# Reading the residual times the norm weight in the first two chunks of four feed-forward stages, and applying the root behind the product

## What is computed

```
def rms_norm(x, g):
    y = x32 * lax.rsqrt(jnp.mean(x32 * x32, axis=-1, keepdims=True) + EPS)
    return (y * g.astype(jnp.float32)).astype(x.dtype)
def modulate(h, shift, scale):
    return h * (1.0 + scale[:, None, :]) + shift[:, None, :]
def swiglu(h, wg, wu, wd):
    return (jax.nn.silu(h @ wg) * (h @ wu)) @ wd

# second block, layer i (the first block has no modulate and no g)
h = modulate(rms_norm(x, ln_ffn1[i]), sh1, sc1)
x = x + 0.5 * g1[:, None, :] * swiglu(h, ffn1_wg[i], ffn1_wu[i], ffn1_wd[i])
...
h = modulate(rms_norm(x, ln_ffn2[i]), sh3, sc3)
x = x + 0.5 * g3[:, None, :] * swiglu(h, ffn2_wg[i], ffn2_wu[i], ffn2_wd[i])
x = rms_norm(x, ln_out[i])
```

## Time and profile before

| what | value |
|---|---|
| median of 3 runs | 1580.49 us (1580.12 to 1580.62) |
| the profiled execution | 1580.53 us, of which the span from the first to the last instruction is 1578.6 us |
| PE busy | 1536.8 us, 97% of the span |
| DVE busy | 1183.6 us, 75% |
| ACT busy | 795.3 us, 50% |
| mean granted clock of PE | 0.989 |

### The profile page before, as it was taken

How to read it: one execution, slowest core, us unless ns; L and a number is a source line. 1 busy time by engine, 2 the same in 40 slices (tenths; PEclk the granted TensorE clock), 3 DMA queues, 4 the chain that set the end, 5 groups by cost and what they waited for, 6 DMA issues and landing times.

```text
span 1578.6 us, 27180 instructions
## 1 busy us (share of the span) xinstructions
PE 1536.8 (97%) x10710; PEld 1417.8 (90%) x10710; DVE 1183.6 (75%) x1435; ACT 795.3 (50%) x931; POOL 13.0 (1%) x33
## 2 busy tenths in 40 slices
PE   6999999899999999999999899999999999999998
PEld 6999998699999999999888799998999989999997
DVE  4788889967888868888867678888655566765555
ACT  5444464464444574444566654445544456454443
POOL 1000000000000000000000000000000000000000
PEclk8999999799999999999999999999999999999999
DMA  6988854238888448888453488886555544545551
GB/s 215 350 310 303 291 159 149 93 127 293 293 303 305 164 156 302 313 303 301 137 165 107 130 278 305 299 286 206 182 182 185 179 164 146 187 160 186 186 186 53
DMA packets 244680, 341.05 MB, mean 216 GB/s; under 512 B 5891, under 2 KB 188315, under 8 KB 244624
## 3 DMA queue, kind: packets, MB, share of 16 engines
q1 hardware_dynamic: 242656, 334.72, 62.3%
q0 software_dynamic: 1968, 5.54, 1.0%
HBM read 339.17 MB, written 2.63 MB: 217 GB/s over the span
## 4 chain that ended last, share of the span: by engine, by line
PE 90%; DVE 5%; ACT 3%; issue 1%; DMA 1%; SPq 0%; DVEq 0%; ACTq 0%
PE banks L1400 26%; PE banks L1365 15%; PE banks L1367 14%; PE banks L1366 14%; PE banks L1401 13%; DVE arena L1081 2%; PE banks L1390 1%; PE banks L1386 1%; DVE w_lo L847 1%; PE banks L1511 1%; ACT w_hi L451 1%; PE banks L1387 1%; PE banks L1454 1%; DMA raw<-in_ffn_w_in 1%; DVE xn L1012 0%
## 5 line engine op out<-in xcount | busy, mean ns | idle before, releaser
L847 DVE TENSOR_TENSOR w_lo<-raw,w_hi 128x2048 fp32r<-128x2048 f32 x245 | 560.2, 2288 | 150.9 <-ACT w_hi L451 150.8
L1400 PE MATMUL banks<-xs,w_hi 128*128 128x512 f32 x1728 | 613.1, 399 | 0.0
L451 ACT ACTIVATE w_hi<-raw 128x2048 fp32r<-128x2048 f32 x245 | 466.7, 1907 | 65.1 <-PE banks L1367 48.0
L1401 PE MATMUL banks<-xs,w_lo 128*128 128x256 f32 x1728 | 485.5, 281 | 0.0
L1400 PEld LDWEIGHTS banks<-xs,w_hi 128*128 128x128 f32 x1728 | 324.9, 188 | 78.4
L1401 PEld LDWEIGHTS banks<-xs,w_lo 128*128 128x128 f32 x1728 | 326.6, 189 | 0.0
L1365 PE MATMUL banks<-gu_hi,w_hi 128*128 128x256 f32 x960 | 274.3, 286 | 0.0
L1367 PE MATMUL banks<-gu_hi,w_lo 128*128 128x256 f32 x960 | 271.7, 283 | 0.0
L1366 PE MATMUL banks<-gu_lo,w_hi 128*128 128x256 f32 x960 | 271.6, 283 | 0.0
L933 DVE SCALAR_TENSOR_TENSOR ada_acc<-ada,c_act,ada_acc 128x512 f32<-128x512 f32 x252 | 189.1, 750 | 7.7
L1365 PE MATMUL banks<-xs,w_hi 128*128 128x256 f32 x640 | 185.4, 290 | 1.0 <-DVE xs L854 1.0
(11 more groups left out here) (258 smaller groups left out, 1821.5 us busy)
## 6 DMA issues: line engine op xcount, KB each, us to landing
ada<-in_ada_w SPq DMA_DIRECT2D x72, 1024.0 KB, 5.0
raw<-in_ffn_w_in SPq DMA_DIRECT2D x44, 1024.0 KB, 6.5
raw<-in_ffn_wg SPq DMA_DIRECT2D x44, 1024.0 KB, 5.3
raw<-in_ffn_wu SPq DMA_DIRECT2D x44, 1024.0 KB, 5.2
raw<-in_ffn_wd SPq DMA_DIRECT2D x44, 1024.0 KB, 4.9
raw<-in_ffn_w_out SPq DMA_DIRECT2D x22, 1024.0 KB, 6.1
raw<-in_attn_w_qkv SPq DMA_DIRECT2D x12, 1024.0 KB, 5.1
raw<-in_w_in SPq DMA_DIRECT2D x10, 1024.0 KB, 5.2
```

The costliest lines, as they stand in the source:

```text
L451: act.activation(w_hi[:, s, :], raw[:, s, :], ACT.Copy).then_inc(hi_ready, 1)
L847: dve.tensor_tensor(w_lo[:, s, :], raw[:, s, :], w_hi[:, s, :].bitcast(F32), ALU.subtract)\
L1400: pe.matmul(o, wh[:, k, m], pair[:, :, k, :], start=(k == 0), stop=False, skip_group_check=True)
L1401: ins = pe.matmul(o[:, 0:T], wl[:, k, m], pair[:, 0, k, :], start=False, stop=(k == KT - 1), skip_group_check=True)
```

## The change

In stages 2, 7, 9 and 11 (`DEFER`) the chunks `c0` and `c0+1` no longer read the normed activation but `u`, which is the residual tile times its norm weight, split into high and low in `xs`. ACT makes `xs_hi` straight from `x` (Identity with the weight column as scale and a column of zeros as bias), tile by tile between its squares, and DVE makes `xs_lo` (`u_low`) in the stage before. PE takes `c0` first and the sums of squares after it, into banks 0 and 1; the filling products are gone in these stages. The root is applied at the banks: DVE multiplies the bank of `c0` into `silu_g` and that of `c0+1` into `gu` (`u_scale`). Where there is a shift (stages 7, 9, 11), the `xs` tiles carry two more columns with it, so that the matmuls of these two chunks have 258 columns and the product of shift and weight comes out in column 256 of each bank; DVE copies it to `u_bias`, and it is added inside Silu and inside the product of gate and up. Then the normed tiles are made as before, for the chunks from `c0+2` on, each `xs_hi` tile once PE has read the old one in `c0+1`. `split(c0+2)` moves ahead of the root on both engines, `split(c0+3)` too on ACT, while on DVE `split(c0+3)` stands behind the eight tiles and the second `u_scale`; `split(c0+1)` of DVE moves behind `u` and the sums of squares; the renormed residual of stage 9 moves behind the second gate times up. The rows of `xs` become 258 words for every stage.

```diff
+DEFER = (2, 7, 9, 11)
...
-        xs = sb("xs", [P, 2, KT, T], F32R)
-        xs_hi, xs_lo = xs[:, 0], xs[:, 1]
+        xs = sb("xs", [P, 2, KT, T + 2], F32R)
+        xs_hi, xs_lo = xs[:, 0, :, 0:T], xs[:, 1, :, 0:T]
+        u_bias = sb("u_bias", [P, 2, 2, 1])
...
+        U_TILES = [banks8[:, i:i + 2, 0:T] for i in (4, 6)]
+        U_SHIFTS = [banks8[:, i:i + 2, T:T + 1] for i in (4, 6)]
...
@@ ACT, norm(n)
+                    if d is not None:
+                        scale, shift = norm_cols(d)
+                        if shift is not None:
+                            act.wait_ge(x_ready, 8 * (n - 1) + 1)
+                            act.activation(xs[:, 0, :, T:T + 2], shifts(d), ACT.Copy)
+                        for k in range(KT):
+                            act.wait_ge(x_ready, 8 * (n - 1) + k + 1)
+                            act.activation(xs_hi[:, k, :], x[:, k, :], ACT.Identity, scale=scale(k), bias=zero_col[:, :])\
+                                .then_inc(xhi_ready, 1)
+                            if k in (1, 3):
+                                square(n, k - 1)
+                                square(n, k)
+                        for k in range(4, KT):
+                            square(n, k)
+                        if joint:
+                            for k in range(KT):
+                                plain_square(k)
+                        split(BASE[d] + 2)
+                        split(BASE[d] + 3)
...
                 for k in range(KT):
                     act.wait_ge(t_ready, 8 * SPLIT_NO[n] + k + 1)
+                    if d is not None and k < KT - 1:
+                        act.wait_ge(u_read, (KT - 1) * DEF_NO[n] + k + 1)
+                    elif d is not None:
+                        act.wait_ge(chunks_done, BASE[n] + 2)
...
@@ ACT, ffn(n)
-                split(c0 + 2)
-                silu(0, c0)
+                if n in DEFER:
+                    act.wait_ge(u_scaled, 2 * DEF_NO[n] + 1)
+                    for j in range(2):
+                        half = silu_g[:, j * T:(j + 1) * T]
+                        bias = zero_col[:, :] if norm_cols(n)[1] is None else u_bias[:, 0, j, :]
+                        ins = act.activation(half, half, ACT.Silu, bias=bias)
+                    ins.then_inc(silu_done, 1)
...
@@ DVE
+            def u_low(m, k):
+                scale, shift = norm_cols(m)
+                dve.wait_ge(xhi_ready, SPLIT_AT[m] + k + 1)
+                if k == 0 and shift is not None:
+                    dve.tensor_tensor(xs[:, 1, :, T:T + 2], shifts(m), xs[:, 0, :, T:T + 2].bitcast(F32), ALU.subtract)
+                dve.scalar_tensor_tensor(out=xs_lo[:, k, :], in0=x[:, k, :], scalar=scale(k),
+                                         in1=xs_hi[:, k, :].bitcast(F32), op0=ALU.mult, op1=ALU.subtract)\
+                    .then_inc(xs_ready, 1)
+
+            def u_scale(n, which, out):
+                dve.wait_ge(chunks_done, BASE[n] + which + 1)
+                root = rstd[:, 0:T].unsqueeze(1).to_broadcast([P, 2, T])
+                if norm_cols(n)[1] is not None:
+                    dve.tensor_copy(u_bias[:, which, :, :], U_SHIFTS[which])
+                dve.tensor_tensor(out[:, :].rearrange("p (a n) -> p a n", a=2), U_TILES[which], root, ALU.mult)\
+                    .then_inc(u_scaled, 1)
...
@@ DVE, norm(n), ahead of the wait for the root; and behind it, ahead of the eight tiles
+                if n in DEFER:
+                    split(BASE[n] + 2)
...
+                if n in DEFER:
+                    u_scale(n, 0, silu_g)
...
@@ DVE, ffn(n)
+                if n in DEFER:
+                    dve.wait_ge(gulo_ready, s0)
+                    u_scale(n, 1, gu)
+                    split(c0 + 3)
+                    dve.wait_ge(silu_done, s0 + 1)
+                    dve.wait_ge(u_scaled, 2 * DEF_NO[n] + 2)
+                    for j in range(2):
+                        half = slice(j * T, (j + 1) * T)
+                        bias = zero_col[:, :] if norm_cols(n)[1] is None else u_bias[:, 1, j, :]
+                        ins = dve.scalar_tensor_tensor(out=gu[:, half], in0=gu[:, half], scalar=bias, in1=silu_g[:, half],
+                                                       op0=ALU.add, op1=ALU.mult)
+                    ins.then_inc(gu_ready, 1)
...
@@ DVE, the end of stages 1 and 10 (projected); stages 6 and 7 end alike
                 residual(n, done, ks=range(2, 6), adds=False)
-                split(c + 5)
+                d = deferred(n + 1)
+                for k in range(6):
+                    u_low(d, k)
                 for b in range(2):
                     add_squares(n + 1, b)
                 residual(n, done, ks=range(6, KT), adds=False)
+                u_low(d, 6)
+                u_low(d, 7)
                 add_squares(n + 1, 2)
+                split(c + 5)
...
@@ PE
+            def wide_u(s, b, n, first):
+                wh, wl = lin(s, w_hi), lin(s, w_lo)
+                cols_u = T if norm_cols(n)[1] is None else T + 2
+                for k in range(KT):
+                    hi, lo = (xs[:, h, k, 0:cols_u] for h in range(2))
+                    halves = [(bank[b + 2 * nb][:, 0:cols_u], slice(nb * P, (nb + 1) * P)) for nb in range(2)]
+                    if first:
+                        pe.wait_ge(xhi_ready, SPLIT_AT[n] + k + 1)
+                    for o, m in halves:
+                        pe.matmul(o, wh[:, k, m], hi, start=(k == 0), stop=False, skip_group_check=True)
+                        pe.matmul(o, wl[:, k, m], hi, start=False, stop=False, skip_group_check=True)
+                    if first:
+                        pe.wait_ge(xs_ready, SPLIT_AT[n] + k + 1)
+                    for o, m in halves:
+                        ins = pe.matmul(o, wh[:, k, m], lo, start=False, stop=(k == KT - 1), skip_group_check=True)
+                    if not first and k < KT - 1:
+                        ins.then_inc(u_read, 1)
+                return ins
...
+                if n in DEFER:
+                    arrived(c0)
+                    pe.wait_ge(x_ready, 8 * (n - 1 - JOINT[n]) + 4)
+                    wide_u(c0 % SLOTS, GATE, n, True).then_inc(chunks_done, 1)
+                    norm(n - JOINT[n], within=True)
+                    arrived(c0 + 1)
+                    wide_u((c0 + 1) % SLOTS, UP, n, False).then_inc(chunks_done, 1)
+                    arrived(c0 + 2)
+                    pe.wait_ge(u_scaled, 2 * DEF_NO[n] + 1)
+                    wide((c0 + 2) % SLOTS, GATE, xs_hi, xs_lo, (xhi_ready, xs_ready, SPLIT_AT[n] + 8))
+                    arrived(c0 + 3)
+                    pe.wait_ge(u_scaled, 2 * DEF_NO[n] + 2)
+                    wide((c0 + 3) % SLOTS, UP, xs_hi, xs_lo)
```

More of the change, by code:

```diff
@@ L67 @@
 TOTAL = sum(c for _, c in STAGES)
+DEFER = (2, 7, 9, 11)
+DEF_NO = [sum(m in DEFER for m in range(n)) for n in range(len(STAGES))]
+SPLIT_AT = [sum(0 if k == "renorm" else 16 if m in DEFER else 8 for m, (k, _) in enumerate(STAGES[:n]))
+            for n in range(len(STAGES))]
 SPLIT_NO = [sum(k != "renorm" for k, _ in STAGES[:n]) for n in range(len(STAGES))]
@@ L482, in norm @@
                     act.wait_ge(ss_ready, n + 1)
-                    act.activation(rstd[:, 0:T], bank[STAT][:, 0:T], ACT.Ln, bias=(eps_sq if joint else eps_col)[:, :])\
+                    total = bank[STAT if d is None else 0][:, 0:T]
+                    act.activation(rstd[:, 0:T], total, ACT.Ln, bias=(eps_sq if joint else eps_col)[:, :])\
                         .then_inc(log_ready, 1)
@@ L550, in ffn @@
                     act.wait_ge(ev("joint_g"), 1)
-                split(c0 + 3)
+                if n not in DEFER:
+                    split(c0 + 3)
                 gu_high(0, None)
@@ L960, in ffn @@
                 gu_mul(1, c0 + 3)
+                if n in DEFER and JOINT[n]:
+                    dve.wait_ge(t_ready, 8 * SPLIT_NO[n] + 8)
+                    dve.wait_ge(rstd_ready, n + 1)
+                    renormed(n - 1, rstd[:, T:2 * T])
                 cl = c0 + 5
@@ L981, in ffn @@
                     low(cs_lo[:, 0:2, :], ub[:, 0:2, :], cs_hi[:, 0:2, :]).then_inc(ev("p_lo"), 1)
-                residual(n, lambda b: (bank_done, 3 * f + b + 1) if b < 3 else (chunks_done, c0 + 33))
+                done = lambda b: (bank_done, 3 * f + b + 1) if b < 3 else (chunks_done, c0 + 33)
+                d = deferred(n + 1) if n + 1 < len(STAGES) else None
+                if d is None:
+                    residual(n, done)
+                else:
+                    residual(n, done, ks=range(4), adds=False)
+                    for b in range(4):
+                        u_low(d, 2 * b)
+                        u_low(d, 2 * b + 1)
+                        if b < 2:
+                            residual(n, done, ks=range(4 + 2 * b, 6 + 2 * b), adds=False)
+                    for b in range(3):
+                        add_squares(n + 1, b)
                 split(c0 + 34)
@@ L1431, in over_two, with norm @@
```

(9 more changed lines are left out.)

85 lines of the change are left out of this document (52 added, 33 removed).

## The result

The changed kernel takes 1560.42 us in the median of 4 runs (1559.31 to 1560.94), the kernel before 1580.47 (1580.12 to 1580.62) beside it: a ratio of 0.987, 95% interval 0.9858 to 0.9881. That is 20.1 us faster; 7.2 were forecast, and the range ended at 1569.4.

What follows compares the result with a forecast made beforehand. PE, busy 97% of the span, was taken as the bound. Of 11.6 us winnable at four stage starts, new waits left 1.90 + 2.45 + 1.45 + 1.38 = 7.2, so 1580.5 - 7.2 = 1573.3 us; range 1569.4 to 1578.0.

Steps and rivals of the forecast that it cites:

- The deferral: Starts of stages 2, 7, 9 and 11: PE runs `c0` before the sums; gain 7.2 us, of 5 to 9, chance 0.62.
- 1.90, 2.45, 1.45 and 1.38: Gains in us forecast for the starts of stages 2, 7, 9 and 11, adding to 7.2.
- The loop of stage 2: From the first 258-column matmul to the loop's first matmul: 31.9 us in stage 2 instead of 33.8.
- ACT's tiles with two columns: ACT's eight Identity instructions with scale and bias columns: 0.50 us apart, as L648, with bounds 0.31 and 0.50.
- The chain behind the root: DVE from root to `split(c0+3)`: 10.0 us (10.8 with shift); each us of root later than 1.5 (0.7) into `c0+1` is lost.
- The waits for `split(c0+3)`: PE idle ahead of `c0+3` in stages 2, 7, 9 and 11: 0.81, 1.03, 0.10 and 1.66 us.
- 5.745: Length in us used for one chunk on PE when working out the stage starts.
- 258 columns cost nothing: 288 matmuls of 258 columns in three stages: 0.0009 us more each, 0.27 us in all.
- Loads, sums and splits are otherwise the same in number: Rest of the kernel: these counts stay unchanged; no time was put on it.
- What costs nothing: Section on work taken as hidden: stage 9's moved `renormed`, ada products, SP's later loads; the root's lateness is the one hinge.
- rival 3: PE pays for the new `xs` shape, 258 columns or 1032-byte row steps: slower, 1590 at half way to 512; chance 0.08.
- matmuls outside these stages change their pace: Named as a sign that the prediction is wrong, for matmuls away from stages 2, 7, 9 and 11; no size or chance.

Runs made afterwards that it cites:

- e12: Changed kernel with ACT's `split(c0+3)` behind Exp and DVE's `split(c0+1)` ahead of all but two low parts, adds behind them; 1560.34 us.
- e9: Kernel before with an unused 128-byte tile ahead of `gu_hi`, so `gu_hi`, `gu_lo` and what lies behind move; 1567.79 us, ratio 0.9919.
- e10: Kernel before with an unused 128-byte tile between `gu_hi` and `gu_lo`, so `gu_lo` and what lies behind move; 1575.23 us, ratio 0.9964.

## Why the prediction was wrong

**The deferral, its mechanism and its sum, were right.** Forecast 7.2 us; measured 7.3 on the new layout, 7.4 on the old place of `gu_hi`, each to about a microsecond, and stage by stage within 0.2 of 1.90, 2.45, 1.45 and 1.38. The loop of stage 2 begins 31.7 us after the start of `c0` (340.35 to 372.01), forecast 31.9. ACT's tiles with two columns go 0.49 to 0.50 apart, as taken from L648. The chain behind the root is the hinge that it was said to be in stages 2 and 11, where e12 shortened it and the start got shorter; in stage 7 its new order cost more in `c0` than it could give.

**Smaller terms.** The waits for `split(c0+3)` were put too high: 0.81, 1.03, 0.10 and 1.66 forecast, 0.63, 0.74, none and 1.32 by the starts of the records, 0.9 us less in sum. On the other side `c0+1` takes 5.83, 5.96, 5.96 and 5.86 us where 5.745 was used, 0.6 us more, and PE comes 0.2 us late to two of the stages. These errors cancel, and no measurement here tells one microsecond of a whole run, so the agreement of the sum to 0.1 is partly luck.

**258 columns cost nothing**, as taken. The timeline of the changed kernel at the start of stage 7:

```profile
893.88 0.28 PE L1519 MATMUL banks<-xs,w_hi 128*128 128x258 f32 x1
894.00 0.28 PE L1520 MATMUL banks<-xs,w_lo 128*128 128x258 f32 x1
894.12 0.28 PE L1519 MATMUL banks<-xs,w_hi 128*128 128x258 f32 x1
```

0.12 apart, as those of 256. The gap that the Trainium skill gives for an isolated matmul (TensorE: Matmul & The Clock Gate, Back-to-back issue gap) would be 110 ns for 258 columns, an estimate by its formula. The trace is some 10 ns above that, and agrees in that two more columns cost next to nothing.

**The step that failed** is "Loads, sums and splits are otherwise the same in number", under "What costs nothing", and the bound that stood beside it: rival 3 let the new shape of `xs` only cost something, per matmul that reads it. Same in number they are, but matmuls far from the four stage starts did change their pace, in the loops of all six feed-forward stages and outside them, since the longer rows and `u_bias` move the tiles behind. That term is absent from the sum, put at nothing without a reason, and it is 12.8 us, more than all that the diff was read for. The text did name, as what would make it wrong, that "matmuls outside these stages change their pace"; it gave no sign, size or chance to it. A range with that term in it, unsigned, would have had to reach as far below 7.2 us of gain as above.

**What stays open** is the mechanism. The runs show that PE's pace in the loops hangs on where `gu_hi` and `gu_lo` lie, in steps as small as 32 bytes and not at 512 or 1024, that the matmuls on `xs` and `w_hi` take part though these lie where they lay, and that the clock is not it. Why a matmul that reads none of the moved tiles gets faster is not shown. If it were an interaction of the reads of one chunk with those of the next, a shift in time might have changed it; only one was tried. Moving the weights or `xs` in place of `gu_hi` and `gu_lo` was not tried, so whether their own place counts or their distance from the others is open too.

## What to carry to other kernels

A diff that changes the size of one tile moves all tiles behind it. Before a gain or a loss is credited to the new work, run the kernel with the new sizes and the old work, and the old kernel with an unused tile of the same size: here that was 64% of the result. In a kernel bound by PE, it is worth trying a few unused bytes ahead of the moving operands, and reading the mean ns of the largest matmul group, which is 399 before and 393 in e9. That group alone does not tell all: with `gu_lo` alone moved (e10) it stays at 399, though the run gains 5.6 us, so the length of a loop's step should be read as well. As for the deferral: what precedes a norm can be filled with the product itself, and the price is then the chain behind the root, down to the next split of weights.

## What the runs showed of the hardware

Matmuls with no wait, of one shape and count, at a granted clock of 1.00 in the window that was read, ran 1.5% apart (613.1 and 603.8 us for 1728 of 512 columns) by nothing but the place of other tiles in SBUF. In whole runs: 128 bytes 12.7 us of 1580, 32 bytes 9.7, 512 and 1024 bytes none. Rows of 258 words in place of 256 gave 3.3 us by themselves; with the better place they left the total as it was, with 4.2 us less gained in the loops (821.0 in e9, 825.2 in e1) and some 5 more outside them, by the two profiled executions. A matmul of two columns between two streams cost 0.13 us (7.0 us for 54), about as much as one of 256, 0.12.
